# One head later: Exp and a Gelu ahead of the scaled copy on ScalarE, a pair's sum ahead of the values on TensorE

## The reference

```
z = x @ w_in                                  # q, k, v (8 heads x 64), GLU value and gate (512 each)
att  = dilated sliding-window attention       # branches (128,1), (512,4), (2048,16), causal
conv = swish(LayerNorm(depthwise conv width 31 (a * sigmoid(g))))
x1 = LayerNorm(ALPHA * x + concat(att, conv) @ w_out)
q  = x1 @ w_query                             # PEER: 8 heads, two 128-wide halves
s  = q . sub_keys; top 16 per side; 16*16 sums; top 16 of them -> 16 experts per head
act = gelu(x1 . u[expert]);  coef = softmax(best) * act
y  = LayerNorm(ALPHA * x1 + sum_k coef_k * v[expert_k])     # 128 experts per token
```

## Time and profile before

| | |
|---|---|
| Median of three executions | 3743.29 us (3739.91 to 3750.01) |
| The profiled execution's own time | 3747.08 us |
| Its span, first to last instruction | 3745.3 us |
| TensorE busy | 69% of the span, granted clock 0.826 of full speed on the mean |
| VectorE busy | 75% |
| ScalarE busy | 18% |
| DMA moved | 1385.68 MB, mean 370 GB/s |
| Expert gathers | 1088, 76.1% of the DMA engines' span |

### The profile page before, as it was taken

One profiled execution on the slowest core, in us unless ns is written; L12 is line 12 of the kernel. 1 busy time (PEld: TensorE's weight loads), 2 busy tenths in 40 slices (PEclk: granted clock), 3 DMA queues, 4 the chain that ended last, 5 costly groups with the idle time before them and its releaser, 6 DMA issues.

```text
span 3745.3 us, 39494 instructions
## 1 busy us (share of the span) xinstructions
PE 2592.0 (69%) x13744; PEld 1193.5 (32%) x13744; DVE 2799.2 (75%) x7472; ACT 681.2 (18%) x1478; POOL 1236.1 (33%) x1092
## 2 busy tenths in 40 slices
PE   7864347736775777677677766776787666779766
PEld 5433124532232223233323332333233322234311
DVE  5177867898789868986897689768976894356965
ACT  1210122002200321032013200320132002121000
POOL 0022212123443444434443434344434432233242
PEclk8987668867887888888788888887888878889889
DMA  9977898979999999999999999999989999999698
GB/s 341 343 296 258 303 371 311 400 278 355 398 417 381 361 381 421 395 367 375 415 391 347 381 421 390 344 369 421 393 336 368 420 409 422 418 420 396 261 384 342
DMA packets 217512, 1385.68 MB, mean 370 GB/s; under 512 B 27417, under 2 KB 38169, under 8 KB 66649
## 3 DMA queue, kind: packets, MB, share of 16 engines
q0 software_dynamic: 156672, 1140.92, 76.1%
q1 hardware_dynamic: 40384, 142.88, 10.4%
q10 hardware_dynamic: 20256, 99.35, 6.7%
HBM read 1369.94 MB, written 80.04 MB: 387 GB/s over the span
## 4 chain that ended last, share of the span: by engine, by line
DVE 30%; PE 26%; DMA 25%; issue 13%; ACT 3%; POOL 2%; ACTq 0%; SPq 0%; DVEq 0%; POOLq 0%
DMA t<-in_expert_uv,t 25%; PE psum L1403 12%; DVE t L1053 8%; PE psum L1250 3%; PE psum L1292 3%; DVE psum L1079 2%; PE psum L1328 2%; POOL t L618 2%; PE psum L1360 2%; DVE t L1064 2%; DVE t L1001 2%; DVE t L999 2%; PE psum L1270 2%; DVE t L1002 2%; DVE t L1000 1%
## 5 line engine op out<-in xcount | busy, mean ns | idle before, releaser
L618 POOL DMA_INDIRECT t<-in_expert_uv,t x1088 | 1235.9, 1136 | 2479.9 <-PE psum L1399 982.0
L1403 PE MATMUL psum<-t,t 64*64 64x512 f32 x4576 | 1323.4, 717 | 652.0 <-DVE t L1064 651.4
L1053 DVE CUSTOM_DVE_ANT_0 t<-t,t 128x1024 f32<-128x1024 f32 x1088 | 1322.2, 1222 | 529.6 <-DMA t<-in_expert_uv,t 520.0
L1399 PE MATMUL psum<-t,t 64*64 64x512 f32 x2592 | 807.9, 753 | 0.0
L1403 PEld LDWEIGHTS psum<-t,t 64*64 64x64 f32 x4576 | 329.0, 154 | 1422.6 <-DVE t L1064 798.4
L770 ACT ACTIVATE t<-t 128x2 f32<-128x2 f32 x544 | 110.6, 203 | 2038.0 <-DVE t L1053 2037.0
L1360 PEld LDWEIGHTS psum<-t,t 128*128 128x128 f32 x2304 | 286.3, 206 | 72.2 <-issue 63.4
L1360 PE MATMUL psum<-t,t 128*128 128x128 f32 (+1 forms) x2304 | 296.6, 291 | 4.8 <-ACT t L740 4.8
L1250 PE MATMUL psum<-t,t 128*128 128x128 f32 (+2 forms) x768 | 269.7, 512 | 6.6 <-DMA t<-in_xT 6.1
L920 DVE SCALAR_TENSOR_TENSOR t<-t,t,t 128x128 f32<-128x128 f32 x840 | 238.0, 346 | 0.0
L1292 PE MATMUL psum<-t,t 128*128 128x64 f32 x576 | 105.9, 348 | 162.7 <-issue 162.2
(11 more groups left out here) (136 smaller groups left out, 2122.2 us busy)
## 6 DMA issues: line engine op xcount, KB each, us to landing
t<-in_wq_t ACTq DMA_DIRECT2D x63, 1024.0 KB, 9.6
out<-in_cache_k_win SPq DMA_DIRECT2D x8, 4080.0 KB, 46.2
out<-in_cache_v_win SPq DMA_DIRECT2D x8, 4080.0 KB, 40.9
t<-in_w_in_t ACTq DMA_DIRECT2D x44, 512.0 KB, 7.5
t<-in_kc_t SPq DMA_DIRECT2D x8, 2560.0 KB, 18.6
t<-in_vc_t SPq DMA_DIRECT2D x8, 2560.0 KB, 14.0
t<-in_expert_uv,t POOLq DMA_INDIRECT x1088, 11.0
t<-in_w_v_t ACTq DMA_DIRECT2D x6, 1024.0 KB, 10.0
```

Of the source, the lines that this page charges most:

```text
L618: pool.indirect_dma_start(ring[:, r, :], None, I["expert_uv"], bass.IndirectOffsetOnAxis(ap=idn[t % 2][:, s:s + 1], axis=0)).then_inc(land ...
L1053: dve.tensor_tensor_reduce(out=ring[:, r, 0:D], in0=x1[t % 2][:, :], in1=ring[:, r, 0:D], scale=1.0, scalar=0.0, op0=ALU.mult, op1=ALU.add ...
L1399: last = pe.matmul(AUX[t][half][NS - NS * a:P - NS * a, :], zt[NS * a:NS * a + NS, k % Z_RING, j, :], vv[NS * a:NS * a + NS, :], start=(c ...
L1403: last = pe.matmul(MAIN[t][half][NS * a:NS * a + NS, :], zt[NS * a:NS * a + NS, k % Z_RING, j, :], vv[NS * a:NS * a + NS, :], start=(c == ...
```

## The change

In the groups of the attention two things are written in another order. On ScalarE, `normalise` of head g-2 moves from quarter 1 to quarter 3 of its group: behind `weights_exp` of head g-1 and behind the Gelu of quarter 3, and still ahead of the copy L694. On TensorE, `values` of head g-2 moves from quarter 1 to quarter 3: behind the pair's sum of quarter 2, and still ahead of the transposes of head g-1. VectorE's, GpSimd's and SyncE's orders are as before, and no semaphore or buffer is changed.

```diff
@@ scalar @@
             def front(m, g, i):
-                if i == 1 and 2 <= g < PH + 2:
-                    normalise(m, g - 2)
                 if i == 2 and 1 <= g <= PH:
                     weights_exp(m, g - 1)
+                if i == 3 and 2 <= g < PH + 2:
+                    normalise(m, g - 2)
                 if i == 3 and 1 <= g <= PH:
                     weights_T(m, g - 1)
```

## The result

| | before | after |
|---|---|---|
| Median of four executions | 3746.65 us | 3627.73 us (3621.01 to 3630.96) |
| Ratio | | 0.9682, 95% interval 0.966 to 0.9704 |
| Profiled execution (its span) | 3747.08 (3745.3) | 3626.55 (3624.7) |
| Mean granted clock of TensorE | 0.826 | 0.849 |
| VectorE's L1061 waiting for the Gelu, whole span | 126.3 us | 12.8 us |

The median before was 3743.29 us of three executions; a fourth at 3750.78 makes it 3746.65. The kernel is 119 us faster, where 76.6 were forecast, and 0.3 us under the low end of the range. The direction was right, the size too small.

The account below looks back on a forecast made before the run. A serial loop through ScalarE was taken to bound the attention of tiles 2 to 7, DMA the rest. Windows fall from 551 to 474.4 us, tiles 0 and 1 zero: 3747.1 - 76.6 = 3670.5, median written 3668, range 3628 to 3724.

Parts of the forecast that it names:

- I give each window the largest of three lengths: Attention windows of tiles 2 to 7: longest of DMA, VectorE and TensorE lengths, sum 474.4 us, 76.6 us less.
- DMA term: Attention of tiles 2 to 7: each window's bytes at 406 GB/s, sum 440.1 us, 110.9 less; the gain's upper bound.
- VectorE at a share of 0.876: Attention of tiles 2 to 7: VectorE's busy time at the highest share a long window shows, 75.5 to 81.0 us.
- TensorE at a share of 0.91: Attention of tiles 2 to 7: TensorE's busy time at the highest share seen, 65.1 to 84.4 us a window.
- the rival with a ceiling of 353: Attention windows: DMA can't pass tile 2's 353 GB/s, so 506.2 us, 44.8 less, time 3698; chance 0.06.
- the bound of 10 either way: Tiles 0 and 1: effect of the change bounded at 10 us either way and taken as zero.
- none at the high clock: TensorE's attention groups: the pair's sum delays values by nothing at the high clock, up to about 1.5 us at the low.
- my slower rival: Attention groups: scores wait for the later scaled copy, about 1.0 us a group over 48 groups, time 3792; chance 0.06.
- TensorE as bound: Attention windows: TensorE can't be busier than 0.77, so lengths sum to 532.7, 18.3 us less, time 3725; chance 0.12.
- Nothing changes: Attention: the wait for the Gelu turns into a wait for landings of gathers, time 3743; chance 0.06.
- the cover in the text: Attention groups: scores' result, 5.1 us after the maximum, precedes VectorE's need some 8.5 us after, hiding the later copy.
- The low end of the range: Whole kernel: 3628 us, reached if DMA bounds the attention, with 3 us for tile 1.

Follow-up runs that it names:

- act_only: ScalarE's half of the change alone (scaled copy behind Exp and Gelu) against the kernel before, TensorE's order as before: 3630.74 us, ratio 0.9711.
- pe_only: TensorE's half of the change alone (values behind the pair's sum of quarter 2) against the kernel before, ScalarE's order as before: 3792.04 us, ratio 1.0135.

## Why the prediction was wrong

The mechanism was right: the loop over values, copy, table load, Exp and Gelu; the wait of L1061 that goes (25.0 to 1.0 us in tile 7); the DMA that comes next. As a gain the miss is a little larger: 3628 lies 115 us under 3743, and 119 were measured. What failed is the step "**I give each window the largest of three lengths**", in two of its three terms.

| shorter by, us | tile 2 | 3 | 4 | 5 | 6 | 7 | sum |
|---|---|---|---|---|---|---|---|
| forecast (largest of three) | 2.0 | 10.5 | 13.4 | 16.9 | 18.2 | 15.6 | 76.6 |
| its DMA term alone | 10.8 | 13.1 | 16.6 | 21.8 | 22.9 | 25.6 | 110.9 |
| measured, by stage | 10.5 | 10.8 | 17.4 | 22.8 | 21.2 | 26.0 | 108.7 |

The two terms count together. With VectorE's share at 0.98 and TensorE's term kept, the same sum gives 91.0 us; with TensorE's term left out and VectorE's kept, 83.9; with both mended, 110.6.

- **VectorE at a share of 0.876.** This was the highest share of a long stretch, but that stretch had a DMA share of 0.98. What it shows is how much VectorE work the stretch had, and no limit of VectorE's. Freed, it reached 0.96 to 0.99. With its busy times at 0.98 the lengths would be 67.5 to 72.4 us, under the DMA's except in tile 2, where they are 0.2 us over it.
- **TensorE at a share of 0.91, with its busy time kept.** The busy time fell from 76.77 to 61.26 us in tile 7's window, as the clock went from 0.85 to 0.98. I had named this in the text on the clock and left it out of the sum. The Trainium skill ("TensorE: Matmul & The Clock Gate", the section on the HAM clock gate) says that sustained work restores the clock; the trace agrees. Whether the new order would keep its gain with the clock at 0.85, no run shows.
- **The DMA term** held: 110.9 against 108.7. The rate rose to 404 to 416 GB/s, so the rival with a ceiling of 353 is out. The Trainium skill ("DMA: Bandwidth & Descriptors", the section on where 436 GB/s comes from) has about 358 GB/s of HBM per core as what binds; the measured rates lie above it, and the measurement decides. The fit of the sum is better than that of its parts, which miss by up to 2.3 us a tile.
- **Tiles 0 and 1** gave 10.5 us where I took zero; the bound of 10 either way nearly held it. The same mechanism was at work there, as the waits of tile 1 show; the step that failed is that I had looked only at TensorE's order and at the DMA share of tile 1. DMA term and this together make 121, and the spans differ by 120.6.
- **TensorE's half.** I wrote that it lets the sum run in idle time and frees ring buffers 4 us earlier. The timeline shows the sum at 2677.98, right behind its `zt`, but it brings little or nothing: `act_only` is as fast within some 10 us. And "none at the high clock" was wrong: in the group shown values start 0.6 us after the maximum's end. That costs nothing in the new order, but in `pe_only` the same delay, longer at the low clock, makes 49 us. That this is near the 3792 of my slower rival is chance, as that rival had another mechanism.
- **The rivals.** TensorE as bound: it is busy for 0.85 of tile 7's window and waits for `zt`. Nothing changes: no dot waits for a landing in tile 7's window, and over its stage they wait 6.6 us, not 25. Slower: scores wait 0.4 us for the copy in that window, so the cover in the text mostly holds.

The low end of the range, 3628, was the DMA's bound with 3 us for tile 1 (3743 less 110.9 less 3 is 3629). It should have lain under the bound by all that tiles 0 and 1 could give. I treated a bound that could be met as one that would not be.

What stays open: what TensorE's higher clock was worth by itself, in either order.

## What to carry to other kernels

An in-order engine that is busy for 18% can still set the pace: ask of each of its instructions what unrelated work stands behind it, and let one that has a long wait stand behind the work that others need first. When a serial loop goes, price what is left by resources that are measured full (here the DMA's rate); the share that another engine happened to reach in a stretch bound by something else is no ceiling for it. A move on one engine can be harmful, free or useful depending on the order of another, so try the halves apart.

## What the runs showed of the hardware

VectorE ran at 0.96 to 0.99 busy beside DMA engines at a share of 1.0 and 404 to 416 GB/s, for 70 us at a time; I had capped VectorE at 0.876 there. The mean clock of TensorE rose by about as much from two added matmuls per group (0.847 to 0.855 with them, 0.829 to 0.838 without, on one chip) as by the change (0.845 to 0.849), with no effect on the time in the first case. In `pe_only` 4.9 us of pairs' sums ran at a granted clock of 0.50, 1.06 us a row instead of some 0.60, on the path that VectorE waited for.
